# Sample rows in a hybrid decoder's mixer: their columns, state products, outputs and output product moved to other places

## The reference, cut to what matters

```python
def mixer(h, conv_buf, S0, w_in, ..., chunked):
    p = h @ w_in
    qkv, new_buf = causal_conv(p[..., :QKV_DIM], conv_buf, conv_w)
    ...
    if chunked:
        o, S = gated_delta_chunked(q, k, v, gdec, beta, S0f)
    else:
        o, S = gated_delta_recurrent(q, k, v, gdec, beta, S0f)
    o_a = (rmsnorm(o, o_norm_g) * jax.nn.silu(gate)).reshape(B, L, W_A)
    vb = rmsnorm(p[..., OFF_V:], v_norm_g)
    o_b = spatial_gate(u, vb, w_s, b_s)
    y = jnp.concatenate([o_a, o_b], axis=-1) @ w_o
    return y, new_buf, S, vb

# the sample rows: one step for each request b and head h (32 states of 128 x 128)
S = S * exp(g)
delta = (v - k @ S) * beta
S = S + outer(k, delta)
o = q @ S
```

## Time and profile before

| | us |
|---|---|
| median of 3 runs | 2586.66 (2585.53 to 2589.39) |
| the profiled execution, its own time | 2582.89 |
| its span, first to last instruction | 2581.2 |
| PE busy | 2468.4 (96%) |
| DVE, ACT, POOL busy | 1387.2, 694.7, 226.5 |
| first instruction of `mix` | 640.03 |
| first instruction of the feed-forward stage | 1071.72 |

### The profile page before, as it was taken

How to read it: one execution, slowest core, us unless ns; L and a number is a source line. 1 busy time by engine, 2 the same in 40 slices (tenths; PEclk the granted TensorE clock), 3 DMA queues, 4 the chain that set the end, 5 groups by cost and what they waited for, 6 DMA issues and landing times.

```text
span 2581.2 us, 36220 instructions
## 1 busy us (share of the span) xinstructions
PE 2468.4 (96%) x13683; PEld 2256.1 (87%) x13683; DVE 1387.2 (54%) x2445; ACT 694.7 (27%) x1424; POOL 226.5 (9%) x411
## 2 busy tenths in 40 slices
PE   5999999998699999699999999999999999999997
PEld 4899999998688888488999999898898998989986
DVE  4445654685556665554444544545745554544455
ACT  4423331211344443221221212122321121211212
POOL 3100011000133333100000000000100000000003
PEclk9999999999699999899999999999999999999999
DMA  4123244322555552521111111121421111111101
GB/s 135 57 74 102 88 128 116 124 74 99 174 158 145 144 145 85 197 62 40 49 49 49 49 48 49 33 65 51 146 62 37 49 49 33 56 42 49 49 25 74
DMA packets 218554, 210.12 MB, mean 81 GB/s; under 512 B 32188, under 2 KB 190240, under 8 KB 215116
## 3 DMA queue, kind: packets, MB, share of 16 engines
q1 hardware_dynamic: 218452, 208.74, 26.4%
HBM read 159.01 MB, written 49.79 MB: 81 GB/s over the span
## 4 chain that ended last, share of the span: by engine, by line
PE 55%; DVE 1%; POOL 1%; issue 1%; ACT 0%; DMA 0%; DVEq 0%; SPq 0%; ACTq 0%; POOLq 0%
PE bank L122 18%; PE bank L124 18%; PE bank L123 18%; PE bank L2049 1%; PE bank L2047 1%; PE bank L2093 0%; DVE f_h_lo L1964 0%; DMA f_up_raw<-in_w_up_dram 0%; POOL ff_rs L101 0%; DVE f_acc L1907 0%; ACT f_relu L140 0%; DVE f_acc L152 0%; POOL ff_rt L109 0%; POOL ff_ms L145 0%; DVE f_xn L1953 0%
## 5 line engine op out<-in xcount | busy, mean ns | idle before, releaser
L1907 DVE TENSOR_TENSOR f_acc<-bank,f_acc 128x512 f32<-128x512 f32 x512 | 351.2, 690 | 296.4 <-PE bank L124 296.3
L122 PE MATMUL bank<-f_h_hi,f_up_lo 128*128 128x344 f32 (+1 forms) x1536 | 490.9, 320 | 4.3 <-DVE f_h_lo L1964 2.9
L124 PE MATMUL bank<-f_h_hi,f_up_hi 128*128 128x344 f32 (+1 forms) x1536 | 489.8, 319 | 0.0
L123 PE MATMUL bank<-f_h_lo,f_up_hi 128*128 128x344 f32 (+1 forms) x1536 | 489.5, 319 | 0.0
L122 PE MATMUL bank<-f_dn_hi,f_z 128*128 128x512 f32 x1024 | 399.3, 390 | 1.9 <-DVE f_acc L1907 1.4
L124 PE MATMUL bank<-f_dn_hi,f_z 128*128 128x512 f32 x1024 | 398.9, 390 | 0.0
L123 PE MATMUL bank<-f_dn_lo,f_z 128*128 128x512 f32 x1024 | 398.8, 389 | 0.0
L122 PE MATMUL bank<-h_hi,w_lo 128*128 128x412 f32 (+3 forms) x1000 | 351.1, 351 | 1.6 <-issue 1.6
L123 PE MATMUL bank<-h_lo,w_hi 128*128 128x412 f32 (+3 forms) x1000 | 350.0, 350 | 0.0
L124 PE MATMUL bank<-h_hi,w_hi 128*128 128x412 f32 (+3 forms) x1000 | 349.7, 350 | 0.0
L1922 DVE TENSOR_TENSOR f_sqr<-f_relu 128x344 f32<-128x344 f32 (+1 forms) x192 | 99.1, 516 | 365.6 <-ACT f_relu L1844 364.1
(11 more groups left out here) (358 smaller groups left out, 2908.6 us busy)
## 6 DMA issues: line engine op xcount, KB each, us to landing
f_up_raw<-in_w_up_dram SPq DMA_DIRECT2D x64, 512.0 KB, 4.6
f_dn_raw<-in_w_down_dram SPq DMA_DIRECT2D x64, 512.0 KB, 3.4
p_dram<-y SPq DMA_DIRECT2D x24, 1024.0 KB, 4.6
w_raw<-in_w_in_dram SPq DMA_DIRECT2D x24, 512.0 KB, 5.8
xres<-in_x_prompt_dram SPq DMA_DIRECT2D x16, 512.0 KB, 4.8
x_dram<-x SPq DMA_DIRECT2D x16, 512.0 KB, 3.0
f_acc<-x_dram SPq DMA_DIRECT2D x16, 512.0 KB, 8.0
out_y_prompt_dram<-f_acc SPq DMA_DIRECT2D x16, 512.0 KB, 2.6
```

Of the source, the lines that this page charges most:

```text
L122: pe.matmul(out, wl, xh, start=start and k == 0, stop=False, skip_group_check=skip)
L123: pe.matmul(out, wh, xl, start=False, stop=False, skip_group_check=skip)
L124: last = pe.matmul(out, wh, xh, start=False, stop=stop and k == n - 1, skip_group_check=skip)
L1907: dve.tensor_tensor(dst, bank, dst, ALU.add).then_inc(s["y_added"], 1)
```

## The change

It moves work of the sample rows to other places; the computation stays.

- The four column loads go to the projection's queue, behind the last x rows; `mix` no longer waits for them.
- On SP in `mix`, constants and the first four slices of `w_o` come ahead of the states.
- `pe_kv` goes behind pass 1 and writes to the bank `turned` (bH) instead of `bank` (bG); `dve_delta` and `dve_outputs` go behind pass 1 and behind the last four cuts of `w_o`.
- `pe_delta` goes into pass 2, behind the first output product of chunk 0, whose wait is now for `qkd_made`; the second half (bH) waits for `delta_copied`. ACT copies delta behind its last cut; its high halves and DVE's low halves of `oT` come behind pass 2 (`act_outputs`, `dve_low`).
- Behind pass 16 PE does outer products 2 to 5 (banks bD, bE, bF, bY) instead of the output product and 2 and 3; behind pass 17 outer products 6 and 7 and then the output product of the sample rows, whose result DVE and ACT add last.

```diff
@@ project, SP
             g_sp(eng, 1)
+
+            eng.dma_start(c.s_vg[:], io["v_norm_g"][0].rearrange("(h p) -> p h", p=P), allow_slow_non_contiguous=True).then_inc(cols_loaded, 16)
+            eng.dma_start(c.s_og[:], io["o_norm_g"][0].rearrange("(p a) -> p a", a=1), allow_slow_non_contiguous=True).then_inc(cols_loaded, 16)
+            eng.dma_start(c.s_w00[:], ...
+            eng.dma_start(c.s_b00[:], ...
             for t in range(NT):
@@ SampleRows
     def pe_kv(self, pe):
         s = self.s
         pe.wait_ge(s["states_loaded"], 16 * H)
-        pe.wait_ge(s["qkd_made"], 1)
+        pe.wait_ge(s["rows_copied"], 2)
         for n in range(NHB):
-            at = 4 * NHB + 2 * n
-            last = pe.matmul(self.bank[:, at:at + 2], self.state(n), self.kq[:, :, n], start=True, stop=True)
+            last = pe.matmul(self.turned[:, 2 * n:2 * n + 2], self.state(n), self.kq[:, :, n], start=True, stop=True)
         last.then_inc(s["kv_ready"], 1)
 
     def pe_delta(self, pe):
         s = self.s
-        pe.wait_ge(s["delta_made"], 1)
-        pe.wait_ge(s["rows_copied"], 2)
-        pe.transpose(self.turned[0:NHB, 0:P], self.delta[:], self.c.ident[:]).then_inc(s["delta_turned"], 1)
         pe.wait_ge(s["o_squared"], 1)
-        pe.matmul(self.bank[:, 6 * NHB:7 * NHB], self.c.ones[:], self.sq[:, 0:NHB], start=True, stop=True).then_inc(s["o_summed"], 1)
+        pe.transpose(self.turned[0:NHB, P:2 * P], self.delta[:], self.c.ident[:])
+        pe.matmul(self.turned[:, 2 * NHB:3 * NHB], self.c.ones[:], self.sq[:, 0:NHB], start=True, stop=True).then_inc(s["o_summed"], 1)
@@
     def act_delta(self, act):
         s = self.s
-        act.wait_ge(s["delta_turned"], 1)
-        act.activation(self.d_rows[:], self.turned[0:NHB, 0:P], ACT.Copy).then_inc(s["delta_copied"], 1)
+        act.wait_ge(s["oms_made"], 1)
+        act.activation(self.d_rows[:], self.turned[0:NHB, P:2 * P], ACT.Copy).then_inc(s["delta_copied"], 1)
+
+    def act_outputs(self, act):
@@ dve_norms
         dve.tensor_tensor(self.prod[:], self.q, self.k, ALU.mult).then_inc(s["prod_made"], 1)
-        dve.wait_ge(s["cols_loaded"], 64)
@@ dve_outputs
         dve.tensor_tensor(self.oa[:], self.oa[:], self.og[:], ALU.mult).then_inc(s["oa_made"], 1)
+
+    def dve_low(self, dve):
         dve.wait_ge(s["hi_made"], 2)
@@ mix
-    outer_banks = [(bD, bE)[u % 2] for u in range(6)] + [bF, bY]
+    outer_banks = [bD, bE, bD, bE, bF, bY, bD, bE]
@@ pe_out
         if (o, half, part) == (0, 0, 0):
 
-            pe.wait_ge(rows.s["oms_made"], 1)
+            pe.wait_ge(rows.s["qkd_made"], 1)
+        if (o, half, part) == (0, 1, 0):
             pe.wait_ge(rows.s["delta_copied"], 1)
-            pe.wait_ge(rows.s["rows_copied"], 2)
@@ pe_pass
         if O:
             pe_out(pe, o, 0, 0)
+        if o == 0:
+            rows.pe_delta(pe)
@@ mix, SP
             load_raw(sp, 0)
-            rows.load_columns(sp)
-            rows.load_states(sp)
             w_sp(sp)
             for k in range(WO_ROOMS):
                 load_w_o(sp, k)
+            rows.load_states(sp)
@@ mix, TensorE
                 if n == 0:
-                    rows.pe_kv(pe)
                     w_pe(pe)
                     pe.wait_ge(ws_copied, 1)
-                    rows.pe_delta(pe)
+                if n == 1:
+                    rows.pe_kv(pe)
                 if n == NCH:
-                    pe.wait_ge(s["ob_sum"], NCH)
-                    rows.pe_project(pe, 0, bF)
-                    pe.wait_ge(s["w_made"], NCH)
-                    rows.pe_project(pe, 1, bY)
                     for u in (2, 3):
                         pe.wait_ge(rows.s["updated"], u - 1)
                         rows.pe_outer(pe, u, outer_banks[u])
-            for u in (4, 5):
-                pe.wait_ge(rows.s["updated"], u - 1)
+                    pe.wait_ge(s["ob_sum"], NCH)
+                    rows.pe_outer(pe, 4, outer_banks[4])
+                    pe.wait_ge(s["w_made"], NCH)
+                    rows.pe_outer(pe, 5, outer_banks[5])
+            for u in (6, 7):
+                pe.wait_ge(rows.s["updated"], u - 3)
                 rows.pe_outer(pe, u, outer_banks[u])
-            pe.wait_ge(rows.s["y_added"], 2)
-            for u in (6, 7):
-                rows.pe_outer(pe, u, outer_banks[u])
+            for half in range(2):
+                pe.wait_ge(rows.s["updated"], 5 + half)
+                rows.pe_project(pe, half, y_banks[half])
@@ mix, VectorE
                 if n == 0:
-                    rows.dve_delta(dve)
                     w_dve(dve)
-                if n == 1:
-                    rows.dve_outputs(dve)
                 if n == NCH:
-                    for half in range(2):
-                        rows.dve_y(dve, half, y_banks[half], y_low[half])
-                    for u in (2, 3):
+                    for u in range(2, 6):
                         rows.dve_update(dve, u, outer_banks[u])
                 if n < 2:
                     for k in range(4 * n, 4 * n + 4):
                         cut_w_o_lo(dve, k)
-
-            for u in range(4, UNITS_S):
+                if n == 1:
+                    rows.dve_delta(dve)
+                    rows.dve_outputs(dve)
+                if n == 2:
+                    rows.dve_low(dve)
+
+            for u in range(6, UNITS_S):
                 rows.dve_update(dve, u, outer_banks[u])
+            for half in range(2):
+                rows.dve_y(dve, half, y_banks[half], y_low[half])
@@ mix, ScalarE
-                if n == 1:
-                    rows.act_delta(act)
-                if n == NCH:
-                    for half in range(2):
-                        rows.act_low(act, half, y_banks[half], y_low[half])
                 if n < 2:
                     for k in range(4 * n, 4 * n + 4):
                         cut_w_o_hi(act, k)
+                if n == 1:
+                    rows.act_delta(act)
+                if n == 2:
+                    rows.act_outputs(act)
+            for half in range(2):
+                rows.act_low(act, half, y_banks[half], y_low[half])
```

More of the change, by code:

```diff
@@ L871, in __init__ @@
         self.og, self.oa, self.ob = (sb("s_" + n, [P, NHB]) for n in ("og", "oa", "ob"))
-        self.vg, self.og_col, self.w00, self.b00 = (sb("s_" + n, [P, H]) for n in ("vg", "og_col", "w00", "b00"))
+        self.vg, self.w00, self.b00, self.og_col = c.s_vg[:], c.s_w00[:], c.s_b00[:], c.s_og[:]
         room = c.taps[:].rearrange("p f r -> p (f r)")
@@ L1043, in dve_norms @@
         dve.wait_ge(s["vb_made"], 1)
-        did(dve.tensor_tensor(by_row(self.ob[:]), by_row(self.vbn[:]), along(self.w00[:], NS), ALU.mult))
-        did(dve.tensor_tensor(by_row(self.ob[:]), by_row(self.ob[:]), along(self.b00[:], NS), ALU.add))
+        did(dve.tensor_tensor(by_row(self.ob[:]), by_row(self.vbn[:]), along(self.w00, NS), ALU.mult))
+        did(dve.tensor_tensor(by_row(self.ob[:]), by_row(self.ob[:]), along(self.b00, NS), ALU.add))
         dve.tensor_tensor(by_row(self.ob[:]), by_row(self.ob[:]), self.rows(4), ALU.mult).then_inc(s["ob_made"], 1)
     def dve_delta(self, dve):
-        s, bank = self.s, self.bank
+        s = self.s
         did = lambda ins: self.own.did(dve, ins)
-        kS_qS = bank[:, 4 * NHB:6 * NHB].rearrange("p (n w) -> p n w", w=2)
+        kS_qS = self.turned[:, 0:2 * NHB].rearrange("p (n w) -> p n w", w=2)
         dve.wait_ge(s["kv_ready"], 1)
@@ L1065, in dve_outputs @@
         dve.wait_ge(s["o_summed"], 1)
-        dve.tensor_scalar(self.ms[:, 0:NHB], self.bank[:, 6 * NHB:7 * NHB], 1.0 / DK, EPS, ALU.mult, ALU.add).then_inc(s["oms_made"], 1)
+        dve.tensor_scalar(self.ms[:, 0:NHB], self.turned[:, 2 * NHB:3 * NHB], 1.0 / DK, EPS, ALU.mult, ALU.add).then_inc(s["oms_made"], 1)
         dve.wait_ge(s["oms_made"], 1)
@@ L1071, in dve_outputs @@
         dve.tensor_tensor(self.oa[:], self.oa[:], self.og[:], ALU.mult).then_inc(s["oa_made"], 1)
+    def dve_low(self, dve):
+        s = self.s
+        did = lambda ins: self.own.did(dve, ins)
         dve.wait_ge(s["hi_made"], 2)
@@ L2195, in build @@
             c.s_qkv, c.s_gate, c.s_gates = keep.sb("s_qkv", [P, NCONV * NS]), keep.sb("s_gate", [P, H, NS]), keep.sb("s_gates", [P, 2 * H * NS])
+            c.s_vg, c.s_w00, c.s_b00 = (keep.sb(n, [P, H]) for n in ("s_vgain", "s_w00", "s_b00"))
+            c.s_og = keep.sb("s_ogain", [P, 1])
             c.alpha, c.negb, c.negg = (keep.sb(n, [P, NCH, H]) for n in ("alpha", "negb", "negg"))
```

23 lines of the change are left out of this document (11 added, 12 removed).

## The result

The kernel after takes 2569.2 us (median of 4 runs, 2565.71 to 2573.57), the kernel before 2586.19 (4 runs, 2585.53 to 2589.39): a ratio of 0.9932, 95% interval 0.992 to 0.9944. Forecast were 2568 us and a range of 2560 to 2577.

What follows compares the result with a forecast made beforehand. PE, busy for 96% of the span, was taken as the bound. Opening 11.6 + drain 5.8 = 17.4 us gave 2565.5 from the profiled execution and 2569.3 from the median; 2568 was said, range 2560 to 2577.

Steps and rivals of the forecast that it cites:

- Columns: Column loads moved to the projection cost nothing there; in the mixer PE leaves for pass 0 8 us earlier.
- Chunk 1's tile: Ahead of pass 1: value tile lands at about 670.0, PE turns it then instead of 682.37, 12.4 us gained.
- Rival (b): Chunk 1's tile gains nothing because the states stand right ahead of it: 2.2 us less, 2570; chance 0.12.
- State products: Behind pass 1: 32 products take 13.2 us, nearly all at half clock, and end at 695.8.
- Rival (a): State products behind pass 1 keep the full clock and end at 689.4: 6.2 us more gained, 2562; chance 0.17.
- Pass 2: First output product takes 4.8 us, no wait for chunk 2's value tile, whose turn at 705.4 gains 9.2 us.
- Squares: In pass 2, DVE's squares of o come at 697.2, ready 3 us before PE asks.
- Low halves: Low halves of the sample outputs behind pass 2: two DVE operations of 0.2 us in DVE's slack.
- Drain: Mixer's end: reordered outer and output products, end set by SP's stores; feed-forward part at 1066.0, 5.8 us gained.
- 0.7 us of spare at the x1 half: In the drain, DVE finishes the x1 half at 1043.4, which PE needs by 1044.1.
- rival (c): Drain gives nothing: clock falls in pass 17 or the output product, PE ends past the stores; 2571 to 2574; chance 0.10.
- Rival (d): SP is held at each load ahead of chunk 1's tile, which lands 28 us later: slower, 2596; chance 0.03.

Runs made afterwards that it cites:

- states_late: The kernel after with the four state loads moved on SP's queue from ahead of chunk 1's tiles to behind them; 2563.06 us, ratio 0.9908.
- interleaved: The kernel after with the 32 state products spread among the 12 matmuls of the first output product; 2572.75 us, ratio 0.9947.
- late_low_xres: states_late with DVE's two low-half operations later in pass 3 and the first residual load behind chunk 2's tiles; 2559.78 us, ratio 0.9897.
- opening_only: The kernel after with the drain order of the kernel before; 2573.36 us, ratio 0.9948.
- drain_only: The kernel before with the new drain order alone; 2582.17 us, ratio 0.9979; executed again, 2583.48 us, ratio 0.9982.
- values_first: late_low_xres with chunk 1's value and gate tiles issued first and PE's wait for the spatial weights' copy moved later; 2560.02 us, ratio 0.9892.

## Why the prediction came out right

The time and the range hold (2568 said, 2569.2 measured), and the sum to the feed-forward part was 17.4 us against 17.6. Term by term:

- **Columns.** Right: no wait of DVE for them, PE 8.0 us earlier, and nothing to be seen of them in the projection's end (the mixer starts 0.5 us later in this trace; over 14 traces the start lies between 639.68 and 641.17, before and after alike).
- **Chunk 1's tile.** Too high by 1.4 us. The step that failed is "Only the columns are gone, 2.2 us of issue. So the tile lands at about 670.0". The issue is not earlier but at the same distance from the mixer's start (25.79 against 25.18 us), since the states' loads now follow eight other loads on SP's queue and hold it for 9.6 us instead of 5.1. It is 2.8 us later than forecast; the tile then lands 5.5 us behind its issue instead of 7.0, which gives half of that back. Rival (b), 2.2 us less, named their place as the reason; states_late shows that it is, and that 6.5 us lay there.
- **State products.** 11.7 us against 13.2. Behind a pass of busy PE they had 2.2 us at full clock; the forecast had allowed "a moment". Rival (a) falls. The page "TensorE: Matmul & The Clock Gate" of the Trainium skill, section "What's actually happening", says that activity releases the throttle; PE was busy for 8.70 of 8.70 us at clock 0.50 here, and in interleaved for 14.00 of 14.00. Taken as PE's busy time, that rule does not hold here.
- **Pass 2.** First output product 4.8 us, as said. Squares at 697.13, as said, and no wait for the tile of chunk 2. The turn gained 10.2 us against 9.2: the two errors above nearly cancel (1.4 too much, 1.5 + 0.5 too little for the products and pass 1, and some tenths).
- **Low halves.** The step "two DVE operations of 0.2 us in DVE's slack" failed twice: 1.84 us and on the path, 1.3 us of the passes behind. late_low_xres shows both.
- **Drain.** 5.8 said, 6.4 in the profile from the first outer product on. Of these, 0.7 us are not the drain's: opening_only, with the old drain, has them too (56.23 us there, 56.89 before, 50.53 after). That leaves 5.7, or 5.4 counted from the mixer's start, and 4.2 by the medians of these two. Stores set its end, as said: DVE's last addition ends at 1052.14, the feed-forward part begins 6.5 us behind the last store's issue. The 0.7 us of spare at the x1 half held (added at 1031.03, no wait). The fall of rival (c) is real but not in this kernel: drain_only shows it twice, 6.8 us at half clock.
- **Rival (d)** falls: the queue was held by the states for 9.6 us in all, and never for a full landing per load.

That the total fits so well is luck in part: three terms are off by 1.3 to 1.5 us, in both directions, and the drain's by 0.1 to 1.6 us, depending on the measure.

## What to carry to other kernels

When a wait is taken away, look at what stands ahead of the next transfer on the issuing queue: here the order of four loads was worth 6.5 us, more than a third of what the whole change brought, and it took one moved line. Read the length of a small operation beside what POOL does at its new place, not at its old one. And follow every queue past which a step is moved, POOL's too.

## What was not expected of the hardware

- Small products (128 rows of weights, 2 columns, float32) keep PE busy without a gap, and the clock still falls while they run: 1.8 to 2.4 us after their start in eight traces that have them behind pass 1, by themselves or mixed with 512-column matmuls, and 0.5 us after it in values_first.
- In the two kernels that were traced twice, the mixer's stretches at half clock repeat to about 1 us, and they differ between kernels that run the same code there: 3.4 us, 6.8 us or none behind the first two outer products, 6.8 us or none from the fourth of the next four on. A difference of 2 to 3 us in such a place can come from the pairing of the kernels and not from the edit.
- DVE's small operations on 128x32 last 0.18 to 0.19 us beside an idle POOL and up to 1.31 us (a step of the outputs' root, at 702.09 in the kernel after) beside a busy one.
- A gain ahead of a stretch at half clock can be lost in it: values_first turned 3.0 us earlier and was 1.0 us later one pass on.

The fastest versions of the study are late_low_xres, 0.9897 of the kernel before (0.988 to 0.9913), and values_first, 0.9892 (0.9876 to 0.9909), which can't be told apart; the kernel after has 0.9932. Not tried: spreading the state products over the later passes, two at a time, which would need room for their results outside the two banks that they use.
